# Rotary positions: changing the halves over by DMA within SBUF in place of a matmul

## The reference, cut to what matters

```
def _apply_rope(t, cos, sin):
    t32 = t.astype(jnp.float32)
    t1, t2 = jnp.split(t32, 2, axis=-1)
    rot = jnp.concatenate([-t2, t1], axis=-1)
    return (t32 * cos + rot * sin).astype(t.dtype)

q_d = _apply_rope(to_heads_d(dq), cos, sin)
k_d = _apply_rope(to_heads_d(dk), cos, sin)
```

## Time and profile before

| | |
|---|---|
| median of 3 runs | 3517.3 us (3516.41 to 3517.88) |
| time of the profiled execution | 3521.87 us |
| its span | 3520.1 us |
| mean granted TensorE clock, as a share of full speed | 0.989 |
| busy in the span: TensorE, weight load | 3449.7 us, 2780.7 us |
| busy in the span: DVE, ACT, POOL | 1224.2 us, 1255.4 us, 1517.9 us |

### The profile page before, as it was taken

One profiled execution on the slowest core, in us unless ns is written; L12 is line 12 of the kernel. 1 busy time (PEld: TensorE's weight loads), 2 busy tenths in 40 slices (PEclk: granted clock), 3 DMA queues, 4 the chain that ended last, 5 costly groups with the idle time before them and its releaser, 6 DMA issues.

```text
span 3520.1 us, 39187 instructions
## 1 busy us (share of the span) xinstructions
PE 3449.7 (98%) x16124; PEld 2780.7 (79%) x16124; DVE 1224.2 (35%) x2103; ACT 1255.4 (36%) x1924; POOL 1517.9 (43%) x706
## 2 busy tenths in 40 slices
PE   8999999998999999999999999999999999999998
PEld 5777887887888888887777888888887778888776
DVE  3265783532221134211553111121114652111544
ACT  4524323433322333223444222322233543222544
POOL 4222444555544444455414444444445234444332
PEclk9999999999999999999999999999999999999999
DMA  7211233432333323333112323232332022223211
GB/s 269 66 54 55 72 109 113 156 144 78 112 129 133 99 95 140 135 93 108 55 34 94 100 95 94 90 105 96 93 96 93 28 75 93 99 90 102 70 62 55
DMA packets 99295, 341.19 MB, mean 97 GB/s; under 512 B 11372, under 2 KB 11756, under 8 KB 98957
## 3 DMA queue, kind: packets, MB, share of 16 engines
q1 hardware_dynamic: 98352, 336.97, 28.9%
q10 hardware_dynamic: 764, 1.72, 0.1%
HBM read 336.02 MB, written 2.10 MB: 96 GB/s over the span
## 4 chain that ended last, share of the span: by engine, by line
PE 94%; ACT 2%; DVE 2%; POOL 1%; DMA 1%; issue 1%; SPq 0%; DVEq 0%; ACTq 0%
PE ps L1183 26%; PE ps L1185 26%; PE ps L1184 26%; PE ps L1202 2%; PE ps L1204 2%; PE ps L1203 2%; PE ps L1484 2%; PE ps L1511 1%; PE ps L1497 1%; PE ps L1399 1%; PE ps L1269 1%; POOL t L2662 1%; PE ps L1413 0%; PE ps L1239 0%; DMA t<-in_w_ada 0%
## 5 line engine op out<-in xcount | busy, mean ns | idle before, releaser
L2662 POOL TENSOR_TENSOR t<-t,t 128x1024 fp32r<-128x1024 f32 (+2 forms) x588 | 1362.8, 2320 | 1802.0 <-ACT t L1579 1801.3
L1183 PE MATMUL ps<-t,t 128*128 128x512 f32 (+1 forms) x4048 | 1607.6, 397 | 17.8 <-POOL t L2662 9.2
L1185 PE MATMUL ps<-t,t 128*128 128x512 f32 (+1 forms) x4048 | 1585.0, 392 | 0.0
L1184 PE MATMUL ps<-t,t 128*128 128x512 f32 (+1 forms) x4048 | 1580.2, 390 | 0.0
L1183 PEld LDWEIGHTS ps<-t,t 128*128 128x128 f32 x4048 | 764.7, 189 | 185.8 <-issue 15.6
L1185 PEld LDWEIGHTS ps<-t,t 128*128 128x128 f32 x4048 | 763.2, 189 | 167.4
L1184 PEld LDWEIGHTS ps<-t,t 128*128 128x128 f32 x4048 | 764.3, 189 | 158.2 <-issue 1.4
L1579 ACT CAST t<-t 128x1024 fp32r<-128x1024 f32 (+2 forms) x588 | 584.3, 995 | 577.6 <-PE ps L1185 424.9
L2455 DVE TENSOR_TENSOR t<-t,ps 128x512 f32<-128x512 f32 x110 | 75.6, 687 | 534.3 <-PE ps L1185 518.5
L1648 ACT CAST t<-t 128x512 fp32r<-128x512 f32 x158 | 97.0, 622 | 401.4 <-DVE t L2455 361.5
L1835 ACT ACTIVATE t<-t 128x512 f32<-128x512 f32 x88 | 55.6, 632 | 313.1 <-DVE t L2448 313.1
(11 more groups left out here) (285 smaller groups left out, 2353.4 us busy)
## 6 DMA issues: line engine op xcount, KB each, us to landing
t<-in_w_f1i SPq DMA_DIRECT2D x88, 512.0 KB, 3.3
t<-in_w_f2i SPq DMA_DIRECT2D x88, 512.0 KB, 3.3
t<-in_w_ada SPq DMA_DIRECT2D x72, 512.0 KB, 4.4
t<-in_w_ffi SPq DMA_DIRECT2D x44, 512.0 KB, 3.6
t<-in_w_f1o SPq DMA_DIRECT2D x32, 512.0 KB, 3.5
t<-in_w_f2o SPq DMA_DIRECT2D x32, 512.0 KB, 3.5
t<-in_w_gate SPq DMA_DIRECT2D x24, 512.0 KB, 4.0
t<-in_w_out SPq DMA_DIRECT2D x48, 256.0 KB, 2.6
```

Source lines behind the costliest of these rows:

```text
L1183: e.matmul(out, wh[:, at], X.hi[c][:, 0:N], start=c == first, stop=False)
L1184: e.matmul(out, wh[:, at], X.lo[c][:, 0:N], start=False, stop=False)
L1185: m = e.matmul(out, wl[:, at], X.hi[c][:, 0:N], start=False, stop=c == final)
L2662: e.tensor_tensor(k.WL[:, n % NHL, 0:w], k.raw[:, j % NRAW, 0:w], f(k.WH[:, n % NHL, 0:w]), ALU.subtract).then_inc(*k.rest.inc(('rest', j) ...
```

## The change

The matmul goes, and so do its matrix in the constants, its PSUM bank and the wait on it. SP gets a `rope`: it takes the buffer of `rope_ring`, waits for the tile and copies it in four DMAs of 32 rows x 2 KB with the halves exchanged. DVE multiplies the buffer in place by a table of sines in which rows of the first half are negated. DVE and POOL both wait until the copies have landed (`turned half`), where they waited for the matmul.

```
-CONSTS = [..., ('nB', 128), ('rot', 128), ('hmean', 128), ('causal', 128)]
+CONSTS = [..., ('nB', 128), ('hmean', 128), ('causal', 128)]
...
-    cs = np.stack([np.cos(emb), np.sin(emb)], axis=1).astype(np.float32)
+    sign = np.where(i % 64 < 32, -1.0, 1.0).astype(np.float32)[:, None]
+    cs = np.stack([np.cos(emb), sign * np.sin(emb)], axis=1).astype(np.float32)
...
 class Sync
+    def rope(self, L, n):
+        k, e = (self.k, self.e)
+        m = self.take(rope_ring(k, L), 'turn', L, n)
+        self.wait_ge('diff in', L, n)
+        turned = load(k, f'turned {n}')
+        for p in (0, 64):
+            e.dma_start(m[p:p + 32, :], k.DQ[p + 32:p + 64, n, :]).then_inc(*turned.inc(by=16))
+            e.dma_start(m[p + 32:p + 64, :], k.DQ[p:p + 32, n, :]).then_inc(*turned.inc(*([('turned half', L, n)] if p else []), by=16))
...
 class Tensor
-    def rope(self, L, n):
-        k, e = (self.k, self.e)
-        b = self.take(k.banks, 'rot', L, n)
-        self.wait_ge('diff in', L, n)
-        e.matmul(b, const(k, 'rot'), k.DQ[:, n, :], start=True, stop=True).then_inc(*k.filled.inc(('filled', ('rot', L, n))))
...
 class Vector
     def rope(self, L, n):
         k, e = (self.k, self.e)
-        m = self.take(rope_ring(k, L), 'turn', L, n)
+        m = rope_ring(k, L).of(('turn', L, n))
         self.wait_ge('load', 'cs', L)
-        self.wait_ge('filled', ('rot', L, n))
-        e.tensor_tensor(m, self.bank('rot', L, n), k.CS[:, 1, :], ALU.mult).then_inc(*k.dve.inc(('rope sine', L, n), ('free', ('rot', L, n))))
+        self.wait_ge('turned half', L, n)
+        e.tensor_tensor(m, m, k.CS[:, 1, :], ALU.mult).then_inc(*k.dve.inc(('rope sine', L, n)))
...
 class Pool
     def rope(self, L, n):
         k, e, x = (self.k, self.e, self.k.DQ[:, n, :])
         self.wait_ge('load', 'cs', L)
-        self.wait_ge('filled', ('rot', L, n))
+        self.wait_ge('turned half', L, n)
         e.tensor_tensor(x, x, k.CS[:, 0, :], ALU.mult).then_inc(*k.pool.inc())
         self.settle()
         self.wait_ge('rope sine', L, n)
```

More of the change, by code:

```diff
@@ L24 @@
 NCOL = _o
-CONSTS = [('ident', 128), ('one', 128), ('mean', 128), ('cols', 4), ('triF', 128), ('triB', 128), ('sufF', 128), ('sufB', 128), ('allS', 128), ('csF', 128), ('csB', 128), ('mF', 128), ('mB', 128), ('nF', 128), ('nB', 128), ('rot', 128), ('hmean', 128), ('causal', 128)]
+CONSTS = [('ident', 128), ('one', 128), ('mean', 128), ('cols', 4), ('triF', 128), ('triB', 128), ('sufF', 128), ('sufB', 128), ('allS', 128), ('csF', 128), ('csB', 128), ('mF', 128), ('mB', 128), ('nF', 128), ('nB', 128), ('hmean', 128), ('causal', 128)]
 CON = {}
@@ L54, in shape_constants @@
     c['causal'] = np.where(t <= s, 0.0, NEG)
[L55 to L60, removed]
     c['hmean'] = same / 64.0
```

## The result

| | before | after |
|---|---|---|
| median, us | 3517.24 (3516.41 to 3517.88, 4 runs) | 3548.16 (3541.73 to 3553.7, 4 runs) |
| profiled execution, us | 3521.87 | 3541.73 |
| mean granted clock in it | 0.989 | 0.986 |

The ratio is 1.0083 (1.007 to 1.0097), which is +29 us (25 to 34). Slower, as forecast with 0.92, but by more: the median stands at the upper edge of the range of 3526 to 3548 (3548.16; by the ratio, 3546.5 against the first 3517.3), beyond the main case's own 3530 to 3543.

The account below looks back on a forecast made before the run. TensorE, with 94% of the chain, was taken to bound the kernel. Per layer +12.6 (idle) + 2.2 (clock) - 5.2 (matmuls saved) = +9.6, so +19.2 for both: profiled 3541.1, median 3536.5 us, range 3526 to 3548.

Parts of the forecast that it names:

- main case: Copies queue behind forget and TensorE idles before dqk1 in each layer: +19 us, range 3530 to 3543, chance 0.62.
- the removal: Seven of a layer's eight rotation matmuls save 0.86 us each, 6.0 a layer, 12.0 in all; the first gains nothing.
- the second copy just covered: Tile 4's copy: POOL waits 1.7 us for it, but TensorE's slow dqk1 matmuls just cover this.
- Steps 1 to 5: Layer 0, from SP's forget issues through loads, copies, landing and POOL's work: dqk1 starts 12.6 us later.
- Step 4: Landing of tile 0's copies behind the fv0 and fv1 loads: 1657.5, low 1655.2, high 1659.5.
- step 5: After landing, POOL's two rope products and its part of dqk1 take 5.2 us; TensorE starts dqk1 at 1662.8.
- The clock behind the idle time: After the idle before dqk1, TensorE runs partly at its lower rate: 2.2 us added a layer.
- The other six of a layer cost nothing: Copies of the tiles other than 0 and 4, including those in attend, make TensorE wait for nothing.
- 1.2 are covered: Tile 6 in attend: DVE stands 1.2 us for the copy, within 6 us of slack before TensorE's use.
- -5.2: Saving per layer from six rotation matmuls of 0.86 us, on the tiles after tiles 0 and 4.
- the dearer case: Issues of 1.0, landing at 1659.5, DVE and POOL held up by 0.7: 3543 to 3546, chance 0.20.
- the median, 4.6 below that execution: The changed kernel's median would lie 4.6 us below its profiled execution of 3541.1, at 3536.5.

Follow-up runs that it names:

- cum_later: The changed kernel with SP's 16 DMAs of forget moved behind the copies of tile 5: 3519.72 us, ratio 1.0004 to the kernel before.
- keep04: The changed kernel with tiles 0 and 4 by matmul again, the other six of a layer by copies: 3513.02 us, ratio 0.9982 to the kernel before.
- no_rot: The kernel before without rotation matmuls and without copies, the sine product taking the tile as it is: 3504.83 us, ratio 0.9962 to the kernel before.
- dve_later: The changed kernel with DVE's and POOL's products of tile 0 behind diff_in of tile 1, of tile 4 behind the lambda products: 3519.29 us, ratio 0.9998.

## Why the prediction was right, and where it was off

**Right: the mechanism of the loss.** The copies stand behind the 16 DMAs of `forget` in SP's queue, POOL's rope behind the copies, the part of dqk1 behind rope. cum_later takes the first link away, with the two loads, and A falls by 11.3 and 13.6 us; keep04 takes it away by not needing it, and A is back at 23.99. Right too: the removal (no_rot, 5.25 against 5.2), the first matmul worth nothing (0.82 became 1.67), and the second copy just covered: POOL waits 1.61 for it (1.7 predicted), and its part of dqk5 ends at 1665.9, TensorE starting dqk5 at 1666.08, 0.36 us after the last start of dqk1 where 0.23 is usual.

**Steps 1 to 5, from SP's start on forget.** The last copy was issued 13.63 us after it (13.76 predicted; the pace was 0.63, not 0.67). Landing came at 17.2, predicted 16.5: 3.6 us from the last issue in place of 2.7. POOL needed 5.4, not 5.2. So dqk1 starts 1.0 us later than predicted, 13.6 instead of 12.6 behind before, counted from dv2. Step 4 is the one mis-sized, by 0.8. Its reason was right: the copies of tile 4, and the median of all, landed in 2.0; tile 0's, with two loads right ahead, took 3.6, and in layer 1 of cum_later, with no load right ahead, 2.15. Its price for the loads, 0.7, was too low; they cost about 1.5. In step 5 POOL's cosine product took 1.77 in place of 1.30 to 1.48; the reason stands below.

**The clock behind the idle time.** A grew by 15.35; the idle time, 14.32, less the matmul, 0.86, and 0.09 of the lambda wait gives 13.37, so 2.0 remain for the slower rate, 2.2 predicted. Most of it is seen directly: the first eight distances of starts take 3.42 us (1658.87 to 1662.29), where 1.8 are usual. Of the stretch behind the idle time, the view by engines: its length, busy time (count) of TensorE, weight load, DVE, ACT and POOL, the granted clock (0.71, where the prediction looked for one near 0.5), DMA:

```profile
1658.87:1664.50 5.63, 5.63 (x18) 4.52 (x19) 0.69 (x1) 0.00 (x0) 4.00 (x3) 0.71 0.37 116
```

**Wrong: "The other six of a layer cost nothing", "1.2 are covered".** They cost 1.9 a layer (B of after 133.70, of no_rot 131.81), so -5.2 was -3.4. The count had the copies land in time for DVE, which they nearly did, and took the product behind as 0.69. It isn't:

```profile
L2494 DVE TENSOR_TENSOR t<-t,t x16: 693/1734/2511, 1653.4 to 2757.0; 128x512 f32<-128x512 f32 x16
```

The same for before, from PSUM:

```profile
L2495 DVE TENSOR_TENSOR t<-ps,t x16: 690/692/693, 1641.0 to 2733.7; 128x512 f32<-128x512 f32 x16
```

Minimum, median and maximum in ns: 693, 1734 and 2511 after, 690, 692 and 693 before. What holds it up is shown by tile 3 in after, DVE's timeline, then POOL's:

```profile
1726.33 2.51 DVE L2494 TENSOR_TENSOR t<-t,t 128x512 f32<-128x512 f32 x1 [1.59 <-DMA t<-t]
1728.76 0.68 DVE L2510 TENSOR_REDUCE t<-ps 128x1 f32<-128x512 f32 x1
```

```profile
1725.89 2.40 POOL L2661 TENSOR_TENSOR t<-t,t 128x1024 fp32r<-128x1024 f32 x1 [4.52 <-ACT t L1578]
```

The product starts while POOL is at its weight part and ends 0.55 us after POOL's end (1728.84 against 1728.29). For tiles 1, 2, 6 and 7 the same distance is 0.55, 0.55, 0.54 and 0.55, with durations of 1.84, 2.41, 1.00 and 2.06, and in layer 1 all five again have 0.55. In before tile 3's product also starts inside POOL's part (DVE's timeline, then POOL's), and takes 0.69:

```profile
1716.75 0.69 DVE L2495 TENSOR_TENSOR t<-ps,t 128x512 f32<-128x512 f32 x1 [2.07 <-PE ps L1474]
```

```profile
1715.85 2.35 POOL L2662 TENSOR_TENSOR t<-t,t 128x1024 fp32r<-128x1024 f32 x1 [4.26 <-ACT t L1579]
```

Nor is it the DMAs into the buffer that slow the product: no_rot has no copies, only the tile in SBUF in place of the bank, and its product of tile 4 starts 0.07 us behind POOL's part and ends 0.54 after it (DVE, then POOL).

```profile
1643.71 2.87 DVE L2489 TENSOR_TENSOR t<-t,t 128x512 f32<-128x512 f32 x1 [2.85 <-POOL t L2713]
```

```profile
1643.64 2.40 POOL L2656 TENSOR_TENSOR t<-t,t 128x1024 fp32r<-128x1024 f32 x1
```

Behind tile 3's product in DVE's queue stand the row maxima, behind these ACT's exponentials, and the PSUM bank that they free is the one that TensorE waits 0.84 for at 1730.55. The Trainium skill, "SBUF — State Buffer", section "Who interferes with whom", has the rule: a VectorE instruction with two SBUF inputs shares an interface with a GpSimd instruction that reads SBUF, and the one that comes second is blocked until the first is through; with at most one SBUF input it isn't. The traces agree, with 0.55 us from POOL's end to the product's end. At tiles 0 and 4 POOL is the one that comes second, 0.04 us behind DVE: its cosine product took 1.77 and 1.78 us against 1.48 and 1.30 before. The prediction put such a hold-up, at 0.7, into the dearer case only, and only at tiles 0 and 4. DVE also stands idle for the copy, 1.2 to 2.3 us for each of the four tiles in `attend`, but it stood 0.7 to 2.5 us for the matmul before. Counted from lambda, tile 3's product starts 53.6 us behind it, in before 54.5, so the copy isn't the later one; without the hold-up it would end 1.8 us sooner, more than the wait of 0.84. That makes the hold-up the likely cause of the larger part of the 1.9 us. No kernel was run in which one is there without the other.

**Wrong: "the median, 4.6 below that execution".** The sum was right for the profiled executions, 19.9 against 19.2, but partly by luck: the layers cost 24.4, 5.2 more than predicted (1.5 in A, 3.7 in B), and the profiled execution of after gained 4.9 elsewhere. And the profiled execution was the fastest of its kernel, so that the median lay 6.4 above it and not 4.6 below. By ratio the change costs 29 us (25 to 34). Of this 24.4 are in A and B of the profiled pair; the other 5 or so aren't located. The profiled executions of after have a mean clock of 0.986 and the slower ones 0.982 to 0.985, and where in them the lower clock falls stays open.

## What to carry to other kernels

Before an operation on an idle-looking engine takes a matmul's place, follow every in-order queue that it enters: here the DMA queue had 10.8 us of small issues ahead, and POOL and DVE each had unrelated work behind the new wait; moving one wait uncovered the next. Count a saving by place: the change loses by two of its eight tiles, and with those two left as matmuls it is faster than both (0.9982, 0.9973 to 0.999). Whether the copies would do better when issued from another engine's queue wasn't tried. Ask also where the operands now lie: a VectorE product that read PSUM and now reads SBUF twice stands behind GpSimd's.

## What the runs showed of the hardware that wasn't expected

- A VectorE product of 128 x 512 with both inputs in SBUF took up to 2.51 us beside a GpSimd product, against 0.69 with one input in PSUM; in each layer five ended 0.54 to 0.55 us after GpSimd's end, and one of no_rot, where no copies write the buffer, took 2.87.
- Four copies of 32 rows x 2 KB within SBUF were issued 0.63 us apart, as 8-row ones within SBUF at 0.67, so the cost of such an issue hardly depends on the number of rows:

```profile
L1112 SPq DMA_DIRECT2D t<-t x32: 507/581/592, 1647.9 to 2754.3; - x32
```

- Landing took 2.0 us for most of them, counted from the last issue, and 3.6 for the first tile of a layer, which has two loads of 512 KB right ahead; without these 2.15 in one layer, and 3.9 in the other, where a 16 KB packet of the instruction queue came between; behind two DMAs of 128 KB within SBUF and two loads, 5.4.
- Behind an idle time of 14.32 us TensorE's starts were 0.43 us apart and then 0.23; behind one of 1.66 (dve_later, at lambda) seven were 0.43 apart as well, but behind one of 1.67 before dv2 none.
